# Cross-attention over memory in a hybrid decoder layer: the next head's query projection is issued ahead of the current head's softmax

## The reference, cut to what matters

```python
mk, mv = _mem_kv(mem_prompt, g_mem[l], w_mem_kv[l])
xn = rmsnorm(x, g_pre_mix)
# mem_q is a 512-column slice of xn @ w_in
mq = mem_q.reshape(B, T, MEM_HEADS, MEM_HD).astype(F32)
s = jnp.einsum('bthd,bmhd->bhtm', mq, mem_k.astype(F32)) * (MEM_HD ** -0.5)
p = jax.nn.softmax(s, axis=-1)
o_mem = jnp.einsum('bhtm,bmhd->bthd', p, mem_v.astype(F32)).reshape(B, T, MEM_WIDTH).astype(dt)
```

## Time and profile before

| | us |
|---|---|
| median of 2 runs | 3078.25 |
| the runs | 3057.55, 3098.95 |
| the profiled execution | 3040.71 |
| its span, slowest core (core 5) | 3039.2 |
| spans of the other cores | 2987.3 to 3036.3 |
| TensorE, VectorE, ScalarE, GpSimd busy on core 5 | 1902.8, 1012.1, 940.4, 496.2 |

### The profile page before, as it was taken

The page is one execution under the profiler, slowest core; times in us unless marked ns, Lnnn a source line. Parts: engine busy times, 40 slices in busy tenths (PEclk is TensorE's granted clock), DMA queues, the critical chain, the costliest instruction groups (busy, mean ns, idle before and its releaser), DMA issues.

```text
span 3039.2 us, 40463 instructions; the slowest of 8 cores (2987.3 to 3039.2 us)
## 1 busy us (share of the span) xinstructions
PE 1902.8 (63%) x13236; PEld 1127.4 (37%) x13236; DVE 1012.1 (33%) x1775; ACT 940.4 (31%) x2119; POOL 496.2 (16%) x495
## 2 busy tenths in 40 slices
PE   2466666666666415666404633999662997979778
PEld 1355555555555313443301221444221332323333
DVE  2233333333343234444432520222156212222231
ACT  6244444444444303444302210222134111111111
POOL 0100101001001000000001002333225313232231
PEclk9877776776767657777656766999785887887798
DMA  4300000000000432000025048221217949697591
GB/s 144 56 1 1 1 1 1 1 1 1 1 1 5 87 98 59 1 1 1 1 83 101 0 62 108 22 22 11 49 35 155 111 57 105 69 95 76 73 98 38
DMA packets 259840, 139.45 MB, mean 46 GB/s; under 512 B 210604, under 2 KB 237329, under 8 KB 259508
## 3 DMA queue, kind: packets, MB, share of 16 engines
q0 software_dynamic: 226832, 83.40, 25.3%
q1 hardware_dynamic: 32804, 53.46, 5.7%
HBM read 201.29 MB, written 18.93 MB: 72 GB/s over the span
## 4 chain that ended last, share of the span: by engine, by line
PE 45%; DMA 16%; ACT 12%; DVE 12%; issue 9%; POOL 4%; DVEq 1%; ACTq 0%; SPq 0%; POOLq 0%
PE psb L194 45%; DMA wfi<-w_ffn_in 6%; DVE hS L218 2%; ACT glnv L214 2%; ACT L214 2%; DVE gVb L218 1%; DMA gS<-state_gdn 1%; DMA mVc<-cache_mem_v 1%; POOL gT L218 1%; POOL gD L218 1%; ACT gth L214 1%; DMA mKc<-cache_mem_k 1%; DMA wgd<-w_in 1%; DMA gS0b<-state_gdn 1%; POOL hall L218 1%
## 5 line engine op out<-in xcount | busy, mean ns | idle before, releaser
L194 PE MATMUL psb<-hnT,wfi 128*128 128x512 bf16 (+1 forms) x1760 | 381.4, 380 | 106.1 <-DMA wfi<-w_ffn_in 80.3
L194 PE MATMUL psb<-xnT,wgd 128*128 128x128 bf16 (+2 forms) x2448 | 243.3, 266 | 86.5 <-DVE gvTb L238 35.5
L194 PEld LDWEIGHTS psb<-hnT,wfi 128*128 128x128 bf16 x1760 | 158.0, 105 | 329.5 <-issue 284.5
L194 PEld LDWEIGHTS psb<-xnT,wgd 128*128 128x128 bf16 (+1 forms) x2448 | 197.4, 120 | 112.6 <-issue 109.8
L194 PE MATMUL psb<-xnT,wgate 128*128 128x512 bf16 (+1 forms) x960 | 198.2, 351 | 43.9 <-DMA wgate<-w_in 28.2
L190 POOL DMA_DIRECT2D wfi<-w_ffn_in x176 | 154.2, 878 | 291.8 <-PE psb L194 261.6
L194 PE MATMUL psb<-wfo,actT 128*128 128x512 bf16 (+1 forms) x748 | 196.4, 435 | 4.1 <-DVE fstat L248 4.1
L214 ACT ACTIVATE fth<-psb 128x512 f32<-128x512 f32 x110 | 57.5, 522 | 355.7 <-PE psb L194 355.7
L238 DVE SCALAR_TENSOR_TENSOR fs<-fth,psb 128x512 f32<-128x512 f32 x110 | 65.3, 594 | 300.8 <-ACT fth L214 266.9
L194 PE MATMUL psb<-xnT,whg 128*128 128x256 bf16 (+1 forms) x864 | 119.3, 300 | 67.8 <-DVE hqtT L218 41.4
L218 POOL TENSOR_TENSOR gD<-gGbc,gtok 128x512 f32<-128x512 f32 (+1 forms) x17 | 17.2, 1013 | 852.4 <-DVE gtok L244 852.4
(11 more groups left out here) (266 smaller groups left out, 3345.3 us busy)
## 6 DMA issues: line engine op xcount, KB each, us to landing
wfi<-w_ffn_in POOLq DMA_DIRECT2D x176, 256.0 KB, 5.9
xt<-x_prompt SPq DMA_DIRECT2D x16, 512.0 KB, 3.7
oxt<-x_prompt SPq DMA_DIRECT2D x16, 512.0 KB, 3.3
y_prompt<-fyt SPq DMA_DIRECT2D x16, 512.0 KB, 2.7
wgate<-w_in POOLq DMA_DIRECT2D x24, 256.0 KB, 5.5
wfo<-w_ffn_out POOLq DMA_DIRECT2D x22, 256.0 KB, 16.6
wgd<-w_in POOLq DMA_DIRECT2D x8, 514.0 KB, 17.3
whg<-w_in POOLq DMA_DIRECT2D x8, 512.0 KB, 20.4
```

Of the source, the lines that this page charges most:

```text
L194: return self.emit("pe", lambda h: h.matmul(out, lhsT=lhsT, rhs=rhs, start=start, stop=stop), rk if rk is not None else [lhsT, rhs], wk if ...
```

## The change

The 20 jobs are put into one list, and a job is cut in two: s1(n) is the projection and the copy of q, s2(n) the rest. The loop issues s1(n+1) ahead of s2(n). mET gets a second pair of halves and mrden2 is a two-part buffer for the prompt's reciprocals. The parts of mqT, mET and mrden2 are now named one by one. The banks are dealt out anew: the K matmuls go to PS[2 + 2*par + c] (banks 2 to 5), the V matmuls to PS[6+par], the ones matmuls to PS[par]. The numbers of matmuls, activations, reciprocals and multiplies, and their shapes, stay as they were.

```diff
         qT = A.alloc("mqT", [128, 2, 512], BF16)
-        ET = A.alloc("mET", [128, 2, 512], BF16)
+        ET = A.alloc("mET", [128, 2, 2, 512], BF16)
         rden = A.alloc("mrden", [128, 512], F32)
+        rden2 = A.alloc("mrden2", [128, 2, 512], F32)
         qTs = A.alloc("mqTs", [128, 4, 64], BF16)
-        cnt = [0]
-        for (tok0, W, ntile, TT, is_s) in STS:
-            for h in range(4):
-                par = cnt[0] % 2
-                cnt[0] += 1
-                for k in range(8):
-                    P.mm(PS[par][:, 0:W], wq[:, k, h * 128:(h + 1) * 128], xnT[:, k, tok0:tok0 + W], start=(k == 0), stop=(k == 7),
-                         rk=[KY(wq, k), xnT])
-                if is_s:
-                    P.act(qTs[:, h, :], PS[par][:, 0:64], AF.Copy, scale=128.0 ** -0.5)
-                    continue
-                P.act(qT[:, par, :], PS[par][:, :], AF.Copy, scale=128.0 ** -0.5)
-                for c in range(2):
-                    P.mm(PS[2 + c][:, :], KT[:, h, c * 128:(c + 1) * 128], qT[:, par, :])
-                    P.act(ET[:, c, :], PS[2 + c][:, :], AF.Exp)
-                for c in range(2):
-                    P.mm(PS[4 + par][:, :], Vsb[:, c, h * 128:(h + 1) * 128], ET[:, c, :], start=(c == 0), stop=(c == 1))
-                for c in range(2):
-                    P.mm(PS[6 + par][:, :], ones_bf[:, :], ET[:, c, :], start=(c == 0), stop=(c == 1))
-                P.recip(rden[:, :], PS[6 + par][:, :])
-                P.tt("dve", omemT[:, h, tok0:tok0 + W], PS[4 + par][:, :], rden[:, :], ALU.mult)
+        jobs = [(tok0, W, is_s, h) for (tok0, W, ntile, TT, is_s) in STS for h in range(4)]
+
+        def s1(n):
+            (tok0, W, is_s, h) = jobs[n]
+            par = n % 2
+            for k in range(8):
+                P.mm(PS[par][:, 0:W], wq[:, k, h * 128:(h + 1) * 128], xnT[:, k, tok0:tok0 + W], start=(k == 0), stop=(k == 7),
+                     rk=[KY(wq, k), xnT])
+            if is_s:
+                P.act(qTs[:, h, :], PS[par][:, 0:64], AF.Copy, scale=128.0 ** -0.5)
+            else:
+                P.act(qT[:, par, :], PS[par][:, :], AF.Copy, scale=128.0 ** -0.5, wk=[KY(qT, par)])
+
+        def s2(n):
+            (tok0, W, is_s, h) = jobs[n]
+            par = n % 2
+            if is_s:
+                return
+            for c in range(2):
+                P.mm(PS[2 + 2 * par + c][:, :], KT[:, h, c * 128:(c + 1) * 128], qT[:, par, :], rk=[KT, KY(qT, par)])
+                P.act(ET[:, par, c, :], PS[2 + 2 * par + c][:, :], AF.Exp, wk=[KY(ET, par, c)])
+            for c in range(2):
+                P.mm(PS[6 + par][:, :], Vsb[:, c, h * 128:(h + 1) * 128], ET[:, par, c, :], start=(c == 0), stop=(c == 1), rk=[Vsb, KY(ET, par, c)])
+            for c in range(2):
+                P.mm(PS[par][:, :], ones_bf[:, :], ET[:, par, c, :], start=(c == 0), stop=(c == 1), rk=[ones_bf, KY(ET, par, c)])
+            P.recip(rden2[:, par, :], PS[par][:, :], wk=[KY(rden2, par)])
+            P.tt("dve", omemT[:, h, tok0:tok0 + W], PS[6 + par][:, :], rden2[:, par, :], ALU.mult, rk=[PS[6 + par], KY(rden2, par)])
+
+        s1(0)
+        for n in range(len(jobs)):
+            if n + 1 < len(jobs):
+                s1(n + 1)
+            s2(n)
```

## The result

| | us |
|---|---|
| before, median of 10 runs | 3019.08 (3004.84 to 3098.95) |
| changed, median of 11 runs | 3055.72 (3050.36 to 3161.51) |
| ratio, with its 95% interval | 1.014 (1.0104 to 1.0176) |
| the profiled execution of the changed kernel | 3055.92 |

The change makes the kernel slower by 1.4%, about 42 us, inside the 2% band. Some executions of either kernel run with a lower TensorE clock on the cores of one die or of both and take up to 3.5% longer; the medians and ranges of the table include them, the ratio leaves them out.

The account below looks back on a forecast made before the run. It took the stage as bound by a chain through TensorE and ScalarE, which the reciprocal joins. Loop +52.0, start +1.2 and end +3.2 make +56.4 us; on 3078.25 that gives 3134 us, range 3092 to 3165.

Parts of the forecast that it names:

- The mechanism: Memory attention loop: projection n+1 waits for reciprocal n-1 on their shared bank, about 15 waits of 3.5 to 4 us.
- The clock: TensorE in each loop turn: projection at half clock (3.57 us), the rest at full, after a 3.7 us idle gap.
- Rival (a): TensorE in the loop: clock stays at 1.2 GHz through every turn; +66.6 us, 3145 us; chance 0.12.
- (b): TensorE in the loop: clock stays at 2.4 GHz; turn 8.61 us, +31.5 us, 3110 us; chance 0.09.
- The turn: Memory attention loop: 10.29 us from one reciprocal's end to the next, against 5.55 us before at full clock.
- with a pitch of 0.69 (two in 1.29): ScalarE in each turn: q copy and two exponentials start 0.69 us apart; the two exponentials take 1.29 us.
- The base of the loop: Kernel before, first to last of the 16 reciprocals: 99.87 us, subtracted from the forecast 151.9 us.
- the start: Ahead of the loop: the second projection precedes the first K matmuls, so the first reciprocal comes 1.2 us later.
- the end: Behind the loop: sample projections and transposes follow the last reciprocal, so the next cache load goes out 3.2 us later.
- the level: Whole kernel before: base 3078.25 us, median of two runs 41 us apart, with up to 20 us allowed either way.
- The chances: Whole kernel against before: within 2% 0.60, slower by over 2% 0.39, faster by over 2% 0.01.

Follow-up runs that it names:

- e1_banks: The changed kernel with the banks of before (K into 2+c, V 4+par, ones 6+par), new order kept; ratio to before 0.9877, 2961.84 us.
- e2_serial: The changed kernel with the order of before, s1(n) then s2(n); its banks, second buffers and part names stay; ratio to before 0.9974.
- e6_twice: The changed kernel with each prompt job's reciprocal done twice out of bank n%2; 3099.03 us in one execution, before 3001.89.
- e4_copyout: The changed kernel, but VectorE copies the denominators out of the bank and takes the reciprocal in SBUF; four runs, 2991.78 to 3060.27 us, no ratio.
- e3_names: The changed kernel with mET named as a whole again in the exponentials' writes and the V and ones matmuls' reads; ratio to before 1.0181.

## Why the prediction was right or wrong

**The mechanism was right.** The wait of TensorE for the reciprocal, by way of the bank, is there 16 times at 3.61 us; the wait for the q copy is gone; the later stages only shifted. e1_banks and e2_serial show that it needs both halves of the change, e6_twice and e4_copyout that it has the length of VectorE's hold on the bank.

**The clock was right.** I took the projection at half clock and the rest of the turn at full; the timeline shows 3.56 and 3.22 us for projections and 0.59 for the ones pair. Rival (a), half clock throughout, and (b), full clock, did not come. Without the 3.6 us wait the clock stays at its upper level in e1_banks (1.00), and with a wait of 0.94 us in e4_copyout in about two turns of three, so part of what the wait costs is the clock it takes along: up to 1.7 us a turn, the projection's 3.57 less 1.89. The swing that the Trainium skill names for kernels that cycle banks ("TensorE: Matmul & The Clock Gate", A second HAM failure mode: psum-queue depth-cycling) shows in the timelines of before, of the changed kernel and of six of the cores of e2_serial; the two profiles of e1_banks do not show it, although that kernel cycles banks too.

**The turn was 0.43 us too long.** The forecast was 10.29 us; measured are mostly 9.86. The step that failed in the sum is "with a pitch of 0.69 (two in 1.29)". I took the 0.69 us between two activations of the earlier trace rows for ScalarE's own pace. It was a wait: both exponentials wrote the one name mET, and the change names its parts. The step from copy to exponential I gave the same 0.69, though no row of before shows those two back to back. I had read that edit only as an earlier start of V. Without a wait activations start 0.49 us apart, once between copy and exponential and once between the exponentials, 0.40 us a turn. e3_names brings the 0.69 between the exponentials back. Over 14 turns, of which some took only 9.5 (9.81 on the mean), and the shorter last one (7.44 measured, 7.8 forecast) this makes the loop 144.8 us where 151.9 were forecast.

**The base of the loop** was 99.87 us, of core 5, which of all cores had the shortest; the mean is 102.0. Together: +42.8 us between the reciprocals, not +52.0. Ahead of them the first reciprocal came 0.4 us later after the first q copy (4.36 us against 3.96 on the mean of the cores), not 1.2. The end of the loop in the changed kernel:

```profile
1811.02 3.36 DVE L251 RECIPROCAL mrden<-psb 128x512 f32<-128x512 f32 x1 [3.29 <-PE psb L194]
...
1814.52 1.69 PE L194 MATMUL psb<-xnT,wmq 128*128 128x64 bf16 x24 [3.61 <-DVE mrden L251]
...
1816.05 1.86 PE L198 MATMUL psb<-identbf,mKc 128*128 128x128 bf16 x16
...
1820.78 0.88 POOL L190 DMA_DIRECT2D mKc<-cache_mem_k  x1 [179.92 <-PE psb L198]
```

The cache load goes out 9.76 us after the last reciprocal's start, where I had 9.0 to 10.0 against 6.30 before; but the whole stretch from the last reciprocal to the last use of a value tile grew by 2.1 us on the mean of the cores, from 93.6 to 95.7, not 3.2, and single cores lie up to 4 us from their mean, so this term is rough. The sum by the traces is 0.4 + 42.8 + 2.1 = 45.3 us, and the timed ratio gives 42 (31 to 53); the forecast of 56.4 us was outside. Of the 11.1 us between 56.4 and 45.3 the turns make 7.1, the base 2.1, the start 0.8 and the end 1.1.

**The time missed for another reason: the level.** The second step that failed is "on their scale I predict 3078.25 + 56.4 = 3134.7": 3134 us and the range from 3092 stood on the median 3078.25 of two runs. Over ten runs the kernel before has a median of 3019.08, 59 us lower; with that base the same sum gives 3075.5. That lower level, and not the 11 to 14 us by which the cost of the change was forecast too high, puts the measured 3055.72 under the range: on the base of 3078.25 even the measured 42 us would have given 3120, inside it. The profile held a hint that I did not use: the earlier trace rows shows core 5 with a mean clock of 0.757 and core 0 with 0.787. The stretch of the last phase in the kernel before, first on core 5, then on core 0:

```profile
2355.00:3039.00 684.00, 577.82 (x2508) 239.36 (x2508) 159.81 (x288) 97.99 (x220) 190.31 (x189) 0.82 0.76 80
```

```profile
2347.00:2987.00 640.00, 501.11 (x2461) 218.36 (x2505) 160.04 (x288) 98.03 (x220) 190.16 (x189) 0.96 0.82 85
```

The same work took 684 us at 0.82 and 640 us at 0.96, in a stage that the change does not touch. The difference does not run along the two dies: core 4 took 677 us at 0.83 there, but cores 6 and 7, of the same die, took 650.5 and 646.5 us at 0.95. They had lost their time earlier: from 1900 to 2100 us their clock was 0.82 and 0.84 where all others had 0.97, and they reached the last phase at 2378 and 2390 us, the others between 2340 and 2362. Why the clock was lower on these cores stays open; what counts for the forecast is that even the profiled 3040.71 us was a raised value. The 20 us that I allowed for the level were half of the spread between the two runs, and two runs do not bound it.

**The chances.** Within 2% had 0.60, and so it came out; but the 0.39 for slower rested on a forecast 5 us under the bound, where the measured cost was some 16 to 20 us under it.

## What to carry to other kernels

When work is issued ahead on an engine that goes in order, follow each PSUM bank around the loop: the early writer must not meet the slowest reader of the turn before, or that reader, until then beside the chain, becomes a link of it. A slow operation such as the reciprocal should hold a bank that nothing early needs, or read a copy. And before a gap between two instructions is taken for an engine's pace, look whether they write one name; a change that renames parts removes such waits.

## What the runs showed of the hardware

A reciprocal of 128x512 float32 takes 3.35 or 3.36 us, from PSUM and from SBUF alike, about five times a copy or multiply of that size (0.69). Activations of 128x512 that wait for nothing start 0.49 us apart although each is shown with 0.60 (changed kernel); with a wait for the one before, 0.69 (e3_names). The loop of e1_banks, whose one gap a turn on TensorE is 0.95 us, kept the upper clock (2.4 GHz) on all 8 cores in both profiled sessions, while in e2_serial, at 5.18 us a turn with gaps of 0.89 and 0.68, two cores kept it throughout and six fell to turns of 6.92 for part of the loop.
